# Column evictions ahead of parameter and angle work on ScalarE in a two-layer decoder trunk

## The reference, cut to what matters

```python
for l in range(DEPTH):                       # DEPTH = 2, S = 512, D_MODEL = 1024
    h = rms_norm(x, attn_norm[l])
    proj = h @ w_in[l]
    (nsa_q, nsa_kv, nsa_g, s5_u, gdn_qkv, gdn_a, gdn_b, gdn_z, sb_qkv, merge_logits) = jnp.split(proj, IN_OFFSETS, axis=-1)
    ...
    x = x + merged @ w_out[l]
    x = x + swiglu_ffn(rms_norm(x, ffn_norm[l]), w_gate[l], w_up[l], w_down[l])
```

## Time and profile before

| what | value |
|---|---|
| median of 3 runs | 2208.4 us (2204.76 to 2209.29) |
| the profiled execution | 2207.65 us, span of its trace 2205.9 us |
| TensorE busy | 2062.5 us (94%) |
| VectorE, ScalarE, GpSimd busy | 1209.8, 761.7 and 540.9 us |
| mean granted clock of TensorE | 0.964 of full speed |
| chain that ended last, by engine | PE 74%, DVE 17%, POOL 4%, ACT 2% |

### The profile page before, as it was taken

One profiled execution on the slowest core, in us unless ns is written; L12 is line 12 of the kernel. 1 busy time (PEld: TensorE's weight loads), 2 busy tenths in 40 slices (PEclk: granted clock), 3 DMA queues, 4 the chain that ended last, 5 costly groups with the idle time before them and its releaser, 6 DMA issues.

```text
span 2205.9 us, 25774 instructions
## 1 busy us (share of the span) xinstructions
PE 2062.5 (94%) x10084; PEld 1654.5 (75%) x10084; DVE 1209.8 (55%) x1686; ACT 761.7 (35%) x1156; POOL 540.9 (25%) x304
## 2 busy tenths in 40 slices
PE   7798998889989999999989989888899999999999
PEld 4578976756777888888867879776577778888887
DVE  6635559754338555553366264796533475555422
ACT  4443231264325432222244422313643353322221
POOL 2345027623117000000034350375131250000000
PEclk9899999999989999999999999899999899999999
DMA  5221011221116233333342210122111343333333
GB/s 226 69 87 57 15 48 58 82 81 63 53 62 220 77 115 100 100 96 105 96 149 90 77 48 20 48 72 90 61 69 53 134 153 92 100 96 96 102 101 104
DMA packets 56847, 196.48 MB, mean 89 GB/s; under 512 B 6432, under 2 KB 6688, under 8 KB 54560
## 3 DMA queue, kind: packets, MB, share of 16 engines
q1 hardware_dynamic: 42768, 152.50, 22.1%
q10 hardware_dynamic: 13968, 42.41, 5.0%
HBM read 176.02 MB, written 18.87 MB: 88 GB/s over the span
## 4 chain that ended last, share of the span: by engine, by line
PE 74%; DVE 17%; POOL 4%; ACT 2%; issue 2%; DMA 1%; POOLq 0%; ACTq 0%; SPq 0%; DVEq 0%; PEldq 0%
PE bank L474 19%; PE bank L476 19%; PE bank L475 19%; DVE arena L1759 4%; DVE arena L1754 3%; PE bank L702 2%; PE bank L944 2%; PE bank L682 2%; PE bank L832 2%; PE bank L905 1%; DVE wL L1398 1%; POOL wL L1998 1%; DVE arena L1927 1%; PE bank L692 1%; DVE arena L1437 1%
## 5 line engine op out<-in xcount | busy, mean ns | idle before, releaser
L474 PE MATMUL bank<-hH,wH 128*128 128x512 f32 (+1 forms) x1536 | 624.5, 407 | 49.8 <-ACT pj L1050 19.5
L475 PE MATMUL bank<-hL,wH 128*128 128x512 f32 (+1 forms) x1536 | 609.7, 397 | 0.0
L476 PE MATMUL bank<-hH,wL 128*128 128x512 f32 (+1 forms) x1536 | 608.4, 396 | 0.0
L1998 POOL TENSOR_TENSOR wL<-raw,wH 128x1024 fp32r<-128x1024 f32 (+1 forms) x114 | 281.3, 2473 | 1153.6 <-ACT wH L1047 1153.4
L474 PEld LDWEIGHTS bank<-hH,wH 128*128 128x128 f32 (+1 forms) x1536 | 294.2, 192 | 132.3 <-issue 42.7
L1047 ACT ACTIVATE wH<-raw 128x1024 fp32r<-128x1024 f32 (+1 forms) x276 | 288.0, 1045 | 280.6 <-PE bank L476 216.9
L476 PEld LDWEIGHTS bank<-hH,wL 128*128 128x128 f32 (+1 forms) x1536 | 293.7, 191 | 65.9 <-issue 0.7
L475 PEld LDWEIGHTS bank<-hL,wH 128*128 128x128 f32 (+1 forms) x1536 | 294.7, 192 | 63.1 <-issue 2.6
L1398 DVE TENSOR_TENSOR wL<-raw,wH 128x1024 fp32r<-128x1024 f32 x162 | 214.1, 1322 | 212.4 <-ACT wH L1047 211.7
L1050 ACT ACTIVATE gst<-bank 128x512 f32<-128x512 f32 x64 | 38.2, 597 | 351.3 <-PE bank L476 351.3
L476 PE MATMUL bank<-hidH,wL 128*128 128x512 f32 x352 | 140.4, 399 | 0.0
(11 more groups left out here) (398 smaller groups left out, 2996.6 us busy)
## 6 DMA issues: line engine op xcount, KB each, us to landing
raw<-weights SPq DMA_DIRECT2D x279, 512.0 KB, 3.5
gates<-gst ACTq DMA_DIRECT2D x64, 256.0 KB, 2.3
gload<-gates ACTq DMA_DIRECT2D x16, 1024.0 KB, 7.7
arena<-weights ACTq DMA_DIRECT2D x10, 512.0 KB, 8.2
xT<-x SPq DMA_DIRECT2D x4, 512.0 KB, 5.8
pj<-weights ACTq DMA_DIRECT2D x4, 512.0 KB, 4.0
out<-xT SPq DMA_DIRECT2D x8, 256.0 KB, 3.7
const<-constants SPq DMA_DIRECT2D x1, 1116.5 KB, 6.7
```

Of the source, the lines that this page charges most:

```text
L474: mm(out, a[0], b[0], start=start, stop=False)
L475: mm(out, a[0], b[1], start=False, stop=False)
L476: return mm(out, a[1], b[0], start=False, stop=stop)
L1998: tt_(l, x, h.bitcast(F32), SU).then_inc(slab_taken[i % RING], 1)
```

## The change

ScalarE's instruction list at the start of each layer is rearranged; VectorE's follows. Nothing is computed otherwise.

- In layer 0 `late_tile` becomes eight `late_high` and then eight `late_square`, with one slab split (gdn1) after the fourth square; VectorE does eight `late_low` and then the seven sums. In the hand-over from layer 0 to layer 1 the order stays as it was.
- The small columns' work, `dt5` and `ea` now stand at i == 2 of the loop (in layer 0 that is still ahead of the first eviction, in layer 1 behind that of gdn2).
- `na`, `la` and the four `cmp_w[0]` DMAs stand at i == 3, behind gdn3's eviction; `mag` and the first sines at i == 4, behind gdn4's; `turn4` at i == 6, behind kcvc's.
- VectorE does `xa` and `na` (which give `ab_ready` 1) right behind `late_out(LATE)`, ahead of the rotation and S5 angles.

```diff
-                            late_tile(k, of)
+                            late_high(k, of)
+                        for k in range(KT):
+                            late_square(k, of)
+                            if k == 3:
+                                high_to(RING + 1)
...
-                    a.wait_ge(*of("h_ready", 2 * KT))
-                    for j in range(4):
-                        a.dma_start(cmp_w[0][j], a_w[NALL + 8 * layer + j].rearrange("p (c n) -> p c n", c=4))\
-                            .then_inc(cmp_loaded[0], 16)
-
-                    a.wait_ge(*of("pack_loaded", 16))
-                    act(dt5, prm("ldt"), ACT.Exp).then_inc(q["trig_done"], 1)
-                    a.wait_ge(*of("abc_done", 1))
-                    act(mag, lrdt, ACT.Exp).then_inc(q["trig_done"], 1)
-                    if layer == 0:
-                        act(sinT[:, :], rope_sin, ACT.Sin)
...
-                        if i == 1:
+                        if i == 2:
                             a.wait_ge(*of("sm_ps", 1))
...
+                            a.wait_ge(*of("pack_loaded", 16))
+                            act(dt5, prm("ldt"), ACT.Exp).then_inc(q["trig_done"], 1)
                             step(act(ea, prm("alog"), ACT.Exp))
+                        if i == 3:
                             a.wait_ge(*of("ab_ready", 1))
...
+                            a.wait_ge(*of("h_ready", 2 * KT))
+                            for j in range(4):
+                                a.dma_start(cmp_w[0][j], a_w[NALL + 8 * layer + j].rearrange("p (c n) -> p c n", c=4))\
+                                    .then_inc(cmp_loaded[0], 16)
-                        if i == 3:
+                        if i == 4:
+                            a.wait_ge(*of("abc_done", 1))
+                            act(mag, lrdt, ACT.Exp).then_inc(q["trig_done"], 1)
...
+                        if i == 6:
                             a.wait_ge(*of("abc_done", 2))
...
                     late_out(LATE[layer])
+                    v.wait_ge(*of("pack_loaded", 16))
+                    v.wait_ge(*of("sm_ready", 1))
+                    step(tt_(xa.rearrange("p (t c) -> p t c", t=4), sm_all[:, :, 16:20],
+                             prm("dtb").rearrange("p (t c) -> p t c", t=4), A_))
+                    stt(na, xa, -1.0, xa, M, ALU.min).then_inc(q["ab_ready"], 1)
```

## The result

The changed kernel took 2176.6 us (median of 4 runs, 2171.7 to 2179.0) where the kernel before took 2206.6 beside it (4 runs, 2202.6 to 2209.3): a ratio of 0.9864, with a 95% interval from 0.9846 to 0.9882, or 30.0 us less. A repeat gave 2175.6 and a ratio of 0.9873 (0.9856 to 0.9889), 28 us. Of the 8.7 us between 2185.3 and 2176.6, 1.8 are not the change's: the forecast started from 2208.4 for the kernel before, whose median is 2206.6 with a fourth run. The other 6.9 are gain that the forecast did not have.

The account below looks back on a forecast made before the run. TensorE, busy 94%, was taken as the bound, losing time at late ScalarE evictions and slow matmuls behind them. 23.75 - 0.6 = 23.1 us off 2208.4 gave 2185.3 us, range 2180 to 2194.

Parts of the forecast that it names:

- Part 1, the evictions first: Projections in both layers: earlier evictions by ScalarE end TensorE's stops and slow steps behind them, together 23.75 us.
- Part 2, the angles: ScalarE's wait for VectorE's angles at i == 4, layer 0: kcvc's eviction 0.6 us late, between 0 and 3.
- First rival: Layer 0: angles come later, the wait moves to gdn5; 5 us lost, 2190; chance 0.16 with the table-change rival.
- Part 3, VectorE's debt: VectorE's convolutions begin later, but its room suffices: layer 0 convolutions end near 91, padding 119, need 125.4; no cost.
- the rival on VectorE's debt: Layer 0: convolutions end at 100, padding at 128.5, TensorE waits 3 us for the compression: 2188.5; chance 0.10.
- Part 4, the start: Start of layer 0: sums done at 21.8, TensorE takes them at 23.06; cost 0, up to 1 us, no gain.
- The rest: From z0 on: everything moves up as a block, stop before z1 stays; slow matmuls 1 to 3 us either way, unsummed.
- the forecast's 14.4: Layer 0, start to kcvc's eviction: forecast to come 14.4 us earlier.
- The range: Whole kernel: 2180 (shorter slow stretch and run spread) to 2194 (rivals at 2190, 3 us of lateness, and spread).
- The slower rival: Dense stretch without TensorE's rests: granted clock falls, 4.8 us more per column; six such columns give 2214; chance 0.04.

Follow-up runs that it names:

- l0_only: New order of ScalarE and VectorE in layer 0 alone, start and layer 1 as in the kernel before: 2186.59 us, ratio 0.9926.
- l1_only: New order in layer 1 alone, the rest as in the kernel before: 2192.03 us, ratio 0.9948.
- no_start: Changed kernel with the start of layer 0 as before (square after each high part, sum after each low part): 2177.92 us, ratio 0.9874.
- u_after: Changed kernel, with ScalarE evicting u1's bank ahead of the fifth tanh: 2178.53 us, ratio 0.988.
- z1u_after: Changed kernel, with z1's slab split by GpSimd ahead of the blocks and u1's bank evicted ahead of the fifth tanh: 2176.12 us, ratio 0.9877.
- z1v_after: z1u_after, with ScalarE also evicting the next bank ahead of the sixth tanh and the four squares: 2176.7 us, ratio 0.9881.
- start_only: Kernel before with only the start of layer 0 changed (eight high parts, then eight squares; sums after low parts): 2202.39 us, ratio 0.9994.
- z1_before: Kernel before, with GpSimd splitting z1's slab ahead of the blocks: 2192.15 us, ratio 0.9944.
- z1_after: Changed kernel, with GpSimd splitting z1's slab ahead of the blocks: 2176.41 us, ratio 0.9869.
- z1vg_after: z1v_after, with ScalarE also evicting gdn5's bank before it waits for the angles: median 2179.08 us; ratio 0.9895 without one run of 5139.76.

## Why the prediction was right and wrong

- **Part 1, the evictions first: right.** gdn3 at 44.09 (forecast about 44), kcvc at 63.38 (63.06, or 63.66 with Part 2's lateness) and, in layer 1, 8.7 us (8.75). l0_only and l1_only show the two parts apart, 16.1 and 10.7 us, each with its forecast within the interval.
- **Part 2, the angles: right.** `mag` came at 59.17 (59.2), gdn5's eviction at 61.95 (62.1). The table load for L1161 ran at 55.24, ahead of the wait, and the load at 59.40 was followed by its activation at 60.70, so 1.28 us and no drain; the Trainium skill's 2.66 us ("ScalarE: Activation LUTs", "What ACT_TABLE_LOAD costs") is again not what this kernel shows. What made VectorE late was what had been named, GpSimd's subtraction beside it, in other instructions than thought: one 128x128 `tensor_scalar` and one 128x8 product took 2.3 and 2.2 us. These two give 4.1 us (forecast 4.0); the later begin of the rotation angles gave 0.6 and not 1.3. VectorE's timeline in the changed kernel:

```profile
52.48 2.31 DVE L1476 TENSOR_SCALAR negm<-const 128x128 bf16<-128x128 f32 x1
54.82 0.23 DVE L1477 CAST id<-const 128x128 bf16<-128x128 f32 x1
...
55.50 2.22 DVE L1483 TENSOR_TENSOR small<-pack,small 128x8 f32<-128x8 f32 x1
57.76 0.17 DVE L1484 TENSOR_SCALAR small<-small 128x8 f32<-128x8 f32 x1
```

GpSimd's in the same stretch:

```profile
51.78 2.93 POOL L2010 TENSOR_TENSOR wL<-raw,wH 128x1024 fp32r<-128x1024 f32 x1 [4.51 <-ACT wH L1047]
55.30 2.40 POOL L2010 TENSOR_TENSOR wL<-raw,wH 128x1024 fp32r<-128x1024 f32 x1 [0.59 <-ACT wH L1047]
```

L1476, 0.23 us before, ended at 54.79 with the first (54.71), and L1483, 0.17 before, at 57.72 with the second (57.70). The Trainium skill, "SBUF — State Buffer", "Who interferes with whom", has the rule: a VectorE instruction with two SBUF inputs contends with a GpSimd one that reads SBUF, and so can a `tensor_scalar` in a two-port mode. The second row agrees with the first part of it; the first row would agree with the second part if L1476 ran in such a mode, which the trace does not tell.
- **First rival, in part.** The margin at gdn5's eviction, under 1 us in the forecast, is about -1 where TensorE passes gdn4 at full clock (l0_only, no_start, u_after, z1u_after, z1v_after: stops of 0.93 to 1.19 for L1050). It costs nothing against the forecast, which took gdn4 with its slow steps: eight of them (1.6 us) cost more than this stop.
- **Part 3, VectorE's debt: the size was wrong, and "No cost" with it.** The convolutions ended at 96.2, not near 91, and the padding at 124.9, not 119 (97 and 21.4 make 118.4; the way from the silu's end took 22.8). The need was not 125.4 but 122.8, as TensorE was 17.6 us earlier and not 15. VectorE's idle time ahead of the silu is zero, as forecast, and so is that ahead of the compression. The price was 1.2 us in the first trace, a stop at vsvw through ScalarE's tanh, a way that the rival on VectorE's debt did not name; in the repeat, no_start and l0_only it was nothing. That a lateness of 2 us at the compression cost nothing is luck: the column laid behind ScalarE's copy hid it. In layer 1 the room is there as forecast: VectorE stood 4.99 us ahead of the compression. In layer 0 of the changed kernel neither row has idle time before it:

```profile
96.17 5.90 DVE L1566 SCALAR_TENSOR_TENSOR arena<-arena 128x512 f32<-128x512 f32 x6
```

```profile
124.79 0.28 DVE L1606 TENSOR_TENSOR comp<-comp 128x124 f32<-128x124 f32 x1
```

- **Part 4, the start: right.** start_only and no_start: nothing. The sum-of-squares matmul started at 23.25 (23.06 before).
- **"The rest": this is the step that failed.** It let everything from z0 on move up as a block, kept the stops before z1 as they were, took the slow steps behind them as 1 to 3 us either way, and put all of it at nothing in the sum. The traces show three terms there in layer 0, all of one sign. The stop at L585 is 1.10 to 1.53 us in the four traces with the old order and 0.16 to 0.43 in the five with the new one, which makes 1.3 us with what comes before it, as the blocks meet no convolution now. The stop for z1's slab fell by 0.3. The slow steps in column z1 cost 2.5 to 2.9 us in the old order (11 to 13 steps) and 1.6 in four of the five new traces (7 or 8 steps); from z1's first matmul to L604 this is 1.1 us. In the fifth, the first trace of the changed kernel, there were none, but the stop at vsvw took up the difference. Together 2.7 us. Beside them, kcvc's eviction came on the mean 0.8 us earlier than the forecast's 14.4 (0.3 in the first trace), and layer 1 gave 0.9 more up to L604, of which it isn't shown that the change made it. That is the 4.4 us between 27.5 and 23.1. The other 2.5 of the first result's 30.0 lie elsewhere, and of the repeat's 28 it is only 0.5; they are put down to the clock of single executions, which is argued and not shown.
- **The range** allowed, below, 3 us for the clock and 2 for the spread, from a median of 2208.4. It had nothing for the blocks, nothing for a lower median of the kernel before, and every rival was on the slow side: no story was told in which the change gives more.
- **The slower rival fell.** The granted clock in the dense stretch did not fall: it was 1.00 of full speed from 52 to 68.5 us, and its mean over the span is 0.970, before it was 0.964.

Why the clock falls for 13 steps behind one 2 us stop and for none behind another is not settled. The new order goes with fewer slow steps, and the stop of 12.4 us some 23 us ahead is the plain difference, but no run here has that stop with a z1 stop of 1.85, or the new order with one of 2.11, so the two aren't parted. What is shown is only that the slow steps hang on the stop: without it (z1_before, z1_after, z1u_after, z1v_after) there are none there, and in z1vg_after, with 4.26 us at L585 in its place, there are 8.

## What to carry to other kernels

When an engine waits in order for something that another engine makes, list what is queued behind the wait and move the part that the bound engine needs ahead of it; the sum of the stop and the slow steps behind it is what it gives, and here it could be read from the trace to within a microsecond, up to the end of the moved stretch. Then ask of the engines that keep their old times (here VectorE) how far they now are from the bound one: the same later edit gave 12 us before this change and nothing that could be told after it, and in between VectorE's room of 14 us had become none. Ask too whether such an edit delays that engine itself, as z1's split did. A stop that one only expects to "stay" should be looked at again, since what runs beside it has changed; and a list of rivals should have one in which the change gives more.

## What the runs showed of the hardware

- In layer 0 a stop of 2.11 us on TensorE was followed by 11 to 13 column steps at 1.2 GHz in the old order, and one of 1.85 by 0 to 8 in the new one; two traces of the same kernel differed by 7 steps at the same stop. In layer 1 a stop of 1.67 was followed by 0 to 8 in either order, and one of 7.1 to 7.4 by 6 to 14. In whole traces the slow column steps cost 14.7 to 24.9 us, and two executions of the same changed kernel differed by 3.
- A 0.17 us instruction of VectorE took 2.22 us beside a GpSimd subtraction that had begun 0.2 us before it, and one of 0.23 us took 2.31 beside another: neither ran slower in proportion, each ended within 0.1 us of the other engine's. So the price in these rows was the time that the other had left, whatever the instruction's own size. L1464 (128x16) shows the same, 2.30 us from 45.00, beside a pair of subtractions that ended at 47.26.
- The table load of a waiting activation ran ahead of its wait (55.24, where the activation came at 59.17).
